# A hybrid attention and recurrence block: another order of the norm steps behind the mixing, and earlier splits of the projection weights

## What is computed

```python
u = rms_norm(h, norm_mix_pre) @ w_in
u_sb, u_rw, gate_sb, gate_rw = jnp.split(u, cut, axis=-1)
o_sb = stick_breaking_attention(sq, sk, sv)
...
y = rwkv7_scan(rh, heads(decay), kh, vh, kk, ah)
mu = jnp.mean(y, axis=-1, keepdims=True)
var = jnp.mean(jnp.square(y - mu), axis=-1, keepdims=True)
y = ((y - mu) * lax.rsqrt(var + GN_EPS)).reshape(B, T, RW_WIDTH)
y = y * ln_gain + ln_bias
bonus = jnp.sum(rh * kh * r_k, axis=-1, keepdims=True) * vh
o_rw = (y + bonus.reshape(B, T, RW_WIDTH)) * (jax.nn.sigmoid(xg) @ gate_up)
...
merged = (jax.nn.sigmoid(gate_sb) * (o_sb @ w_branch_sb)
          + jax.nn.sigmoid(gate_rw) * (o_rw @ w_branch_rw))
h = h + rms_norm(merged @ w_out, norm_mix_post)
```

## Time and profile before

| | |
|---|---|
| median of 3 runs | 918.1 us (917.25 to 918.97) |
| profiled execution | 915.49 us, span 913.7 us |
| TensorE busy | 881.7 us, 96% |
| VectorE busy | 470.4 us, 51% |
| ScalarE busy | 410.1 us, 45% |
| POOL busy | 65.6 us, 7% |
| mean granted TensorE clock | 0.995 |
| chain that ended last | TensorE 91%, VectorE 3%, ScalarE 2% |

### The profile page before, as it was taken

How to read it: one execution, slowest core, us unless ns; L and a number is a source line. 1 busy time by engine, 2 the same in 40 slices (tenths; PEclk the granted TensorE clock), 3 DMA queues, 4 the chain that set the end, 5 groups by cost and what they waited for, 6 DMA issues and landing times.

```text
span 913.7 us, 19005 instructions
## 1 busy us (share of the span) xinstructions
PE 881.7 (96%) x8257; PEld 729.6 (80%) x8257; DVE 470.4 (51%) x634; ACT 410.1 (45%) x572; POOL 65.6 (7%) x84
## 2 busy tenths in 40 slices
PE   4899999999999999999999999999999999999997
PEld 3899999876877788776787887888888888888886
DVE  5348767436676745636566554444444444422243
ACT  5335554449878765664354432233333222221231
POOL 1011212011010101022200000000000000000000
PEclk9999999999999999999999999999999999999999
DMA  9231223321111112131276512333333332232221
GB/s 286 81 93 56 84 70 93 115 72 37 37 38 38 38 50 60 38 127 47 69 215 210 174 47 85 99 92 92 92 92 92 92 92 92 93 115 93 93 93 69
DMA packets 109150, 83.34 MB, mean 91 GB/s; under 512 B 2910, under 2 KB 99464, under 8 KB 108824
## 3 DMA queue, kind: packets, MB, share of 16 engines
q1 hardware_dynamic: 109080, 82.29, 29.6%
HBM read 76.51 MB, written 5.77 MB: 90 GB/s over the span
## 4 chain that ended last, share of the span: by engine, by line
PE 91%; DVE 3%; ACT 2%; issue 1%; DMA 1%; SPq 0%; POOL 0%; POOLq 0%; DVEq 0%; ACTq 0%
PE psum L554 48%; PE psum L1747 17%; PE psum L1498 9%; PE psum L1535 6%; PE psum L1672 2%; PE psum L1403 1%; PE psum L1682 1%; PE psum L1790 1%; PE psum L1653 1%; PE psum L1701 1%; DMA w_raw<-in_w_in 1%; ACT w_hi L539 1%; DVE w_lo L544 1%; PE psum L1394 1%; PE psum L1464 0%
## 5 line engine op out<-in xcount | busy, mean ns | idle before, releaser
L554 PE MATMUL psum<-h_hi,w_hi 128*128 128x512 f32 (+1 forms) x736 | 233.6, 353 | 6.8 <-DVE w_lo L544 5.1
L554 PE MATMUL psum<-h_lo,w_hi 128*128 128x512 f32 (+1 forms) x736 | 231.1, 349 | 0.0
L554 PE MATMUL psum<-h_hi,w_lo 128*128 128x512 f32 (+1 forms) x736 | 229.9, 348 | 0.0
L554 PEld LDWEIGHTS psum<-h_hi,w_hi 128*128 128x128 f32 x736 | 129.3, 189 | 28.2 <-DVE w_lo L544 5.7
L544 DVE TENSOR_TENSOR w_lo<-w_raw,w_hi 128x1024 fp32r<-128x1024 f32 x69 | 85.4, 1238 | 127.1 <-ACT w_hi L539 127.1
L554 PEld LDWEIGHTS psum<-h_lo,w_hi 128*128 128x128 f32 x736 | 128.7, 189 | 18.8 <-issue 1.0
L554 PEld LDWEIGHTS psum<-h_hi,w_lo 128*128 128x128 f32 x736 | 129.0, 190 | 18.0
L1349 DVE TENSOR_TENSOR w_lo<-w_raw,w_hi 128x1024 fp32r<-128x1024 f32 x44 | 53.8, 1225 | 132.6 <-ACT w_hi L1026 132.6
L539 ACT ACTIVATE w_hi<-w_raw 128x1024 fp32r<-128x1024 f32 x70 | 73.8, 1055 | 79.4 <-PE psum L1747 63.0
L1026 ACT ACTIVATE w_hi<-w_raw 128x1024 fp32r<-128x1024 f32 x44 | 46.3, 1056 | 69.8 <-PE psum L554 69.8
L1747 PE MATMUL psum<-w_hi,act_hi 128*128 128x512 f32 x144 | 45.7, 389 | 0.0
(11 more groups left out here) (293 smaller groups left out, 1497.2 us busy)
## 6 DMA issues: line engine op xcount, KB each, us to landing
w_raw<-in_w_in SPq DMA_DIRECT2D x42, 512.0 KB, 3.9
w_raw<-in_w_g SPq DMA_DIRECT2D x22, 512.0 KB, 3.7
w_raw<-in_w_u SPq DMA_DIRECT2D x22, 512.0 KB, 3.7
w_raw<-in_w_d SPq DMA_DIRECT2D x22, 512.0 KB, 3.5
w_raw<-in_w_out SPq DMA_DIRECT2D x8, 512.0 KB, 5.5
kept_gates<-gate_raw SPq DMA_DIRECT2D x10, 256.0 KB, 2.7
sig_t<-kept_gates SPq DMA_DIRECT2D x10, 256.0 KB, 3.0
x_in<-in_x SPq DMA_DIRECT2D x4, 512.0 KB, 6.4
```

The costliest lines, as they stand in the source:

```text
L554: mm = nc.tensor.matmul(o, w[:, (w0 + i) * P:(w0 + i + 1) * P], xs[:, k, c0:c1], start=(n == 0), stop=(n == total - 1))
```

## The change

The list `LATE` gets other items in another order. A column add of the norm's bias onto the bonus (`lb`) goes to POOL at the start. Both gate products stand at the start too. The reciprocals are items of their own, one for each channel group, placed between units; the roots of the second round get their own two buffers, so that they need not wait for the reciprocals of the first. The gain is applied by VectorE together with the reciprocal (a scaled multiply), and VectorE also adds the bonus. The squares of the second round move from ahead of unit 1 to behind it. ScalarE's scaling and POOL's sum are gone. In the last branch unit the next two projection units (16 and 17) are split on ScalarE and VectorE ahead of the merge.

```diff
-POST_ITEMS = {"square": ([], ["sq0", "sq1"], [], []),
-              "var": (["var0", "var1"], ["root0", "root1"], ["recip0", "recip1"], []),
-              "gate": (["gate0", "gate1"], ["gain0", "gain1"], ["norm0", "norm1"], ["bonus0", "bonus1"]),
+POST_ITEMS = {"lb": ([], [], [], ["lb0", "lb1", "lb2", "lb3"]),
+              "gates": (["gate0", "gate1"], [], [], []),
+              "square": ([], ["sq0", "sq1"], [], []),
+              "var": (["var0", "var1"], ["root0", "root1"], [], []),
+              "recip0": ([], [], ["recip0"], []), "recip1": ([], [], ["recip1"], []),
+              "norm": ([], [], ["norm0", "norm1", "add0", "add1"], []),
               "out": ([], ["hi0", "hi1"], ["out0", "out1"], ["lo0", "lo1"])}
 
-LATE = [("osb", 0), ("square", 0), ("unit", 0), ("var", 0), ("square", 1), ("unit", 1), ("gate", 0), ("unit", 2),
-        ("var", 1), ("out", 0), ("unit", 3), ("gate", 1), ("unit", 4), ("out", 1), ("unit", 5)]
+LATE = [("osb", 0), ("lb", 0), ("gates", 0), ("gates", 1), ("square", 0), ("unit", 0), ("var", 0), ("unit", 1),
+        ("recip0", 0), ("square", 1), ("var", 1), ("unit", 2), ("recip1", 0), ("unit", 3), ("norm", 0), ("recip0", 1),
+        ("out", 0), ("unit", 4), ("recip1", 1), ("norm", 1), ("unit", 5), ("out", 1)]
...
+WO_FIRST = 2
...
+                if item == "lb":
+                    pool.wait_ge(bonus_back, 16)
+                    for p in range(PAIRS):
+                        g.tensor_scalar(bonus[:, p, :], bonus[:, p, :], vcol[:, V_LB + p:V_LB + p + 1], None,
+                                        ALU.add).then_inc(post_pool, 1)
...
-                        if i:
-                            act.wait_ge(post_dve, upto(POST_DVE, "post", i - 1, f"recip{q}"))
-                        s_.activation(yrs[q][:], bank(6 + q), ACT.Sqrt, bias=small[:, 7:8],
+                        s_.activation(yrs[2 * i + q][:], bank(6 + q), ACT.Sqrt, bias=small[:, 7:8],
...
                         hi_unit(act, u + 2)
+                        if u == U_OUT - 1:
+                            for k in range(2, 2 + WO_FIRST):
+                                hi_unit(act, U_OUT + k)
...
+                if kind in ("recip0", "recip1"):
+                    q = int(kind[5])
+                    dve.wait_ge(post_act, upto(POST_ACT, "post", i, f"root{q}"))
+                    if i:
+                        dve.wait_ge(post_dve, upto(POST_DVE, "post", i - 1, f"norm{q}"))
+                    v_.reciprocal(yrec[q][:], yrs[2 * i + q][:]).then_inc(post_dve, 1)
+                if kind == "norm":
                     for q in range(2):
+                        p = 2 * i + q
+                        dve.wait_ge(post_dve, upto(POST_DVE, "post", i, f"recip{q}"))
+                        v_.scalar_tensor_tensor(y_of(p), y_of(p), vcol[:, V_LG + p:V_LG + p + 1], yrec[q][:],
+                                                ALU.mult, ALU.mult).then_inc(post_dve, 1)
                     for q in range(2):
+                        p = 2 * i + q
+                        dve.wait_ge(post_dve, upto(POST_DVE, "post", i, f"norm{q}"))
+                        dve.wait_ge(post_pool, upto(POST_POOL, "post", 0, f"lb{p}"))
+                        v_.tensor_add(y_of(p), y_of(p), bonus[:, p, :]).then_inc(post_dve, 1)
...
                     lo_unit(dve, u + 2)
+                    if u == U_OUT - 1:
+                        for k in range(2, 2 + WO_FIRST):
+                            lo_unit(dve, U_OUT + k)
...
-                if kind == "gate":
+                if kind == "gates":
```

More of the change, by code:

```diff
@@ L387, in build @@
         yo = [sb(f"y_o{i}", [P, SEQ]) for i in range(2)]
+        yrs += [sb(f"y_rs{i}", [P, SEQ]) for i in range(2, 4)]
         def at(offset, name, shape, dt=F32):
@@ L961, in _ @@
                         hi_unit(act, u + 2)
-            for k in range(KT - 2):
-                hi_unit(act, U_OUT + k + 2)
+            for k in range(2 + WO_FIRST, KT):
+                hi_unit(act, U_OUT + k)
             def tail_root(block, count):
@@ L1247, in _ @@
             for kind, i in LATE:
-                if kind == "var":
+                if kind in ("recip0", "recip1"):
[5 more added lines that the diff above has]
+                if kind == "norm":
                     for q in range(2):
-                        dve.wait_ge(post_act, upto(POST_ACT, "post", i, f"root{q}"))
-                        v_.reciprocal(yrec[q][:], yrs[q][:]).then_inc(post_dve, 1)
-                if kind == "gate":
+                        p = 2 * i + q
+                        dve.wait_ge(post_dve, upto(POST_DVE, "post", i, f"recip{q}"))
+                        v_.scalar_tensor_tensor(y_of(p), y_of(p), vcol[:, V_LG + p:V_LG + p + 1], yrec[q][:],
+                                                ALU.mult, ALU.mult).then_inc(post_dve, 1)
                     for q in range(2):
-                        y = y_of(2 * i + q)
-                        dve.wait_ge(post_dve, upto(POST_DVE, "post", i, f"recip{q}"))
-                        v_.tensor_mul(y, y, yrec[q][:]).then_inc(post_dve, 1)
+                        p = 2 * i + q
+                        dve.wait_ge(post_dve, upto(POST_DVE, "post", i, f"norm{q}"))
+                        dve.wait_ge(post_pool, upto(POST_POOL, "post", 0, f"lb{p}"))
+                        v_.tensor_add(y_of(p), y_of(p), bonus[:, p, :]).then_inc(post_dve, 1)
                 if kind == "out":
                     for q in range(2):
-                        dve.wait_ge(post_pool, upto(POST_POOL, "post", i, f"bonus{q}"))
+                        dve.wait_ge(post_dve, upto(POST_DVE, "post", i, f"add{q}"))
                         dve.wait_ge(post_pe, upto(POST_PE, "post", i, f"gate{q}"))
@@ L1280, in _ @@
                         v_.tensor_sub(mg_lo[:, j, :], mrg_t[0][:], mg_hi[:, j, :].bitcast(F32)).then_inc(mrg_dve, 1)
-            for k in range(KT - 2):
-                lo_unit(dve, U_OUT + k + 2)
+            for k in range(2 + WO_FIRST, KT):
+                lo_unit(dve, U_OUT + k)
             def inverse(b, roots):
```

## The result

The changed kernel takes 926.18 us (median of 4 runs, 925.35 to 928.73) where the kernel before takes 918.4 beside it: ratio 1.0096, 95% interval 1.0075 to 1.0117, so 7.8 us slower. A second set gives 927.56 beside 917.32, ratio 1.0110 (1.0094 to 1.0127), 10.2 us. The profiled execution took 928.73 us, its span 926.9; it is the longest of the four of the first set, 2.5 above their median, while the one before was 2.6 under the median of its set.

What follows compares the result with a forecast made beforehand. TensorE, busy 96%, was taken to bound the kernel through its waits. 10.4 - 1.96 + 3.2 = 11.6 us took the profiled 915.5 to 927.1; 2.6 more for the median gave 929.7 us, range 925.5 to 932.5.

Steps and rivals of the forecast that it cites:

- What bounds, and the order of lists: TensorE is busy 96%, so only its waits count; ScalarE and VectorE run lists in order; 4.4 to 4.7 us winnable.
- (c): Second pair's norm ends under units 4, 5 and half of unit 6: 913.6 us, or 916.0 with the new 2.4; chance 0.05.
- (d): Counters are full by then and the list does not order the steps: about no change; chance 0.03.
- The chain: From unit 3's end to unit 6's second half 24.5 us, 6.3 longer; with unit 3 ending 4.1 later, 10.4 us later.
- Table load ahead of the squares: ScalarE's squares behind a sigmoid might need a function table load of about 1.3 us; none was taken.
- POOL beside VectorE: Two-input VectorE work beside POOL ends late: low half ahead of unit 6 ends 1.09 us after POOL's second subtraction.
- The scaled multiply: Norm on VectorE: scaled multiply costs 0 to 0.3 us in the chain over a plain multiply; 0 was taken.
- The early splits: Projection units 16 and 17 split ahead of the last merge remove TensorE's wait at the third tile: gain 1.96 us.
- The clock: TensorE's clock falls after the 2.4 us wait near the squares and the 8 us wait in unit 6: together 3.2 us.
- the 11.6 of the sum: Whole change: 10.4 later, less 1.96 for the projection, plus 3.2 for the clock, gives 11.6 us slower.
- rival (b): Clock stays low twice as long behind the long wait in unit 6: 931.3 us; chance 0.10.
- rival (a): Clock does not fall after the 2.4 wait, or is low for little behind the long one: 927.0 to 928.1; chance 0.20.

Runs made afterwards that it cites:

- new_order: All steps of the changed kernel in another order, such as squares ahead of unit 1 and both first reciprocals behind unit 0: 912.02 us beside 917.44 before, ratio 0.9949.
- fill_long: Changed kernel plus 28 products that nothing reads in TensorE's long wait in unit 6: 925.34 us beside 917.26 before, ratio 1.0091.
- before_again: The kernel before, unchanged, run and traced a second time: 916.75 us beside 916.41, ratio 0.9995.
- late_only: Changed kernel without the early projection splits, only the new order and the norm on VectorE: 930.88 us beside 917.44 before, ratio 1.0141.
- out_behind: Kernel before in old order with norm on VectorE, bias on POOL, no early splits, first round's out moved behind unit 3: 913.83 us, ratio 0.9966.
- no_second_recip: Changed kernel with the second round's two reciprocals replaced by copies, part of the computation left out: 921.20 us beside 917.32 before, ratio 1.0044.

## Why the prediction was right, and where it was off

- **What bounds, and the order of lists.** Right. Every wait is where it was put: 2.1 for `y_sq` (2.3 said), 2.5 for the low half ahead of unit 6 (2.5), 7.7 for POOL inside unit 6 (8.0), none at the projection. Rivals (c), a chain that ends in time, and (d), no change, are out with these waits. The 4.4 to 4.7 that it said could be won is right too: new_order wins 4.8 in stage and projection.
- **The chain.** Right to 0.1. The end of unit 3 is 0.20 before the sigmoid at 434.11, 433.9; the second half of unit 6 starts at 458.41, 24.5 later, as worked out. Unit 3 itself ends 27.7 behind the first small product, where it was 425.90 - 404.01 = 21.9: 5.8 later, for 4.1 and one fall of the clock said. The 10.4 is what fill_long shows with the clock out of it.
- **Table load ahead of the squares.** There is none: the squares follow the high half at once.
- **POOL beside VectorE.** Right. The low half ended 447.60 - 446.52 = 1.08 behind POOL, 1.09 was taken.
- **The scaled multiply.** A pair took 1.41 and 1.31 and not 1.27, 0.2 in the chain: inside the 0 to 0.3. The column adds took 6.25 for four (6.4 said) and hid.
- **The early splits.** Right: 1.94 to 1.97 by the traces for the 1.96, and 1.3 and 1.8 by the medians, whose intervals leave room for it.
- **The clock, in the traces.** Right in kind, and its size varies. The two falls came where they were put and cost 4.2 and 3.0 in the two traces, for the 3.2. With the projection's gain the traces of the changed kernel are 95.60 - 81.05 - 1.94 = 12.6 and 94.42 - 81.05 - 1.95 = 11.4 over before, for the 11.6 of the sum. In the first the clock was low for 12 products behind the long wait, more than the 8 of one price and less than the two of rival (b).
- **The clock, between medians.** This is the term that was mis-sized. fill_long, whose trace has the chain at full clock, is 8.1 over before; the changed kernel is 7.8 and 10.2 over it. So between medians the clock costs about 0 to 2 us, 1 on average, and not 3.2. Two things were wrong in the step. It counted the fall behind the wait of 2.4 in full, and that fall comes in some executions only. And it added the falls to a median that lies 2.6 over the trace they were worked out from. Some of what such a median holds is other than falls in the stage: the 2.0 of before_again arose ahead of it, and the price of a fall in the feed-forward part is in both traces of before and not in the first of the changed kernel.

The result, 926.2, therefore lies 3.5 under the forecast and inside the range; rival (a), at most one price of the clock with 927.0 to 928.1, is nearer, and the second set's 927.6 is in it. The time alone would thus have pointed to (a), while both traces have both falls.

What stays open: what the executions without a trace hold. Three of the changed kernel's first four ran at a mean granted clock of 0.990 and took 925.4 to 926.2; the traced one ran at 0.988 and took 928.7. Which fall the three lack is not shown. late_only fits this picture: its one execution at 0.990 took 928.1, which is 1.9 to 2.7 over those three, for the 2.0 due, and its other three ran at 0.986 and took 930.1 to 932.3. So the surplus of its median goes with the clock, though its trace places only 1.6 of it.

## What to carry to other kernels

When several engines walk one hand-written list, an item's place in it is a wait: a step behind "unit u" cannot start before unit u ends, even with all its inputs there. Count for each engine what is left on its list behind the last unit that can hide it, and move long steps (here reciprocals of 3.3 us) into the earliest gap of that engine whose inputs are ready. Put a step that waits for a slow partner behind the step that feeds the bottleneck, not ahead of it. In out_behind that one move did as much as the whole new order.

## What the runs showed of the hardware

Two-input operations of VectorE and POOL that run side by side cost time. A single low half that VectorE started beside POOL's work took 1.63 to 1.66 us for 1.23 in the changed kernel, new_order and no_second_recip, and 1.46 in out_behind, where it started later in POOL's work. In all four it ended 1.08 us behind POOL's, which is about its own length: it gained nothing by starting early. POOL lost nothing there, 2.52 to 2.56 for its pair. A reciprocal, which has one input, took its 3.34 beside POOL in new_order. In out_behind the pair of scaled multiplies and the pair of sums ran beside POOL's first pair of low halves. They took 2.44 and 2.38 in place of 1.4 and 1.3, and there POOL lost time too, 3.36 for about 2.5. VectorE's timeline of out_behind (start, duration):

```profile
431.88 2.44 DVE L1259 SCALAR_TENSOR_TENSOR a_r<-a_r,vec_cols,y_rec 128x512 f32<-128x512 f32 x2
434.24 2.38 DVE L1265 TENSOR_TENSOR a_r<-a_r,bonus 128x512 f32<-128x512 f32 x2
```

And POOL's in the same stretch:

```profile
432.11 3.36 POOL L735 TENSOR_TENSOR orw_lo<-y_o,orw_hi 128x512 fp32r<-128x512 f32 x2 [18.29 <-ACT orw_hi L942]
```

And two executions of one kernel can reach a stage 2 us apart with equal work ahead of it, and one wait of 1.66 us can end with a fall of the clock or without, which is another 1.6. So 1 us can be read from the distance inside a stage and hardly from the time.
